# Zeroing the gate map from the mixing stage's DMA queue instead of the routing stage's

## The chip, the cores and the metric

The kernel runs on one core of a Trainium2 chip. The metric is the time of one execution on the device, in microseconds; lower is better. Before the change it is 1831.16 us, the median of three runs (1828.79 to 1844.94).

## What is computed

One layer of a streaming encoder over 512 frames and 16 meta tokens, width 1024: a token mixer (four heads of retention beside eight heads of indexer-selected attention, then one output projection), and PEER, a product-key mixture over 128 x 128 single-neuron experts. Cut to what the change touches:

```python
h += token_mixer(rmsnorm(h, norm_mix), w_in, w_uv, w_out)      # retention | attention, then @ w_out
hn = rmsnorm(h, norm_ffn)
# PEER: each token picks 16 experts in each of 8 heads
q1, q2 = split(einsum('nd,dhk->nhk', hn, w_q), 2)
s1, s2 = q1 @ sub_keys[:, 0], q2 @ sub_keys[:, 1]              # 128 scores each
eidx, gate = top16 of the sums of top16(s1), top16(s2); gate = softmax
a = einsum('nd,ned->ne', hn, u_emb[eidx])
h += einsum('ne,ned->nd', gelu(a) * gate, v_emb[eidx])
out = rmsnorm(h, norm_final)
```

## The kernel before

Matrices of f32 are multiplied in three passes: each operand is split into a high part (ScalarE copies it to a rounded type) and a low part (VectorE or GpSimd subtracts), and TensorE does high times high, high times low and low times high (lines 403 to 405, helper `three_pass`).

The program has five blocks with a barrier between them: `normed_inputs`, `project` (the input projection), `mix_rows` (retention, attention, output projection, second norm; from 244 us to 409 us of the profile), `route` (queries, top 16, gates, the first 24 of 128 tiles of expert products) and `experts` (the other tiles and the sum over them). For three of the four blocks of 128 frames the expert layer is dense: the activations of every expert are kept in DRAM (`up_acts`), and so is a dense map of gates, `gate_map`, of 128 x 128 x 384 numbers or 25 MB. It has to be zero before 384 indirect stores scatter the gates into it. POOL issues those in `experts`, after a wait for the semaphore `zeroed`. The zeros come from one tile of 128 x 384, `zeros`, which `store_zeros` writes out in 32 DMAs (`ZERO_STORES`), each of 128 x 4 x 384 numbers, 786 KB; in one of them each partition writes a piece of 6 KB, and the pieces lie 196,608 bytes apart.

All direct loads and stores are issued by SyncE (SP) into one hardware queue, in the order of the program. Where SP waits for a semaphore, all that it issues later waits too. What sets the order around the change:

- In `mix_rows` SP loads, after the tables, the 16 units of `w_out` (512 columns of 128 rows, 262 KB each) through a ring of four raw tiles, `raw_out`; unit u waits until the low part of unit u - 4 is made (`load_unit`, line 429). Then it loads the residual rows x of a block of frames (`load_rows`, line 953, 524 KB) each time the block's mixed rows have been transposed, waits until the last meta term is added (`meta_added`), and loads query tiles of `peer_wq` (524 KB each, `ts_raw_wq`, line 1518) with the last rows of x between them.
- TensorE works through 36 steps of attention, the blocks of frames in the order 3, 2, 1, 0. From step 11 on, `filler` puts pieces of the output projection between them. `project_half` needs the high and the low part of the mixed rows (`m_lo_done`) and the units of `w_out` (`lo_done`).
- ScalarE (ACT) works strictly in the order of its program. In step 11 that is: exponentials, copy of a result, the high parts of units 11 and 12 of `w_out` (line 437), the high part of the mixed rows (`high_mixed`, line 1401, `x_hi`). In step 12: exponentials, copy, units 13 and 14. After the last step: `high_mixed` of the last block, the high parts of query tiles 0 and 1 (`wq.split_hi`, line 1524), the squares of the last block's first half (`square`, line 1406), which needs x of that block, and then the high parts of the normed rows of the first three blocks (`high_normed`, line 1416). TensorE transposes normed rows (`turn_normed`, line 1114) into five PSUM banks; the sixth transpose of four waits for the first `low_normed` of VectorE (line 1323), which waits for the first `high_normed`.
- In `route` SP alternates loads of query tiles and expert tiles with stores of activations. Before the change the 32 zero fills are there, two behind each of its 16 steps.

The tile `zeros` is filled by one memset of POOL.

## Time and profile before

| | before |
|---|---|
| median of 3 runs | 1831.16 us |
| runs | 1828.79, 1831.16, 1844.94 us |
| the profiled execution, first to last instruction | 1734.2 us |
| mean granted clock of TensorE | 0.998 |
| TensorE busy | 1694.7 us, 98% |
| VectorE, ScalarE, GpSimd busy | 1105.1, 577.1, 927.0 us |
| bytes moved by DMA | 351 MB, 202 GB/s over the span |

The span is that of one profiled execution. The timed runs are about 97 us longer, because they take in what lies around the first and the last instruction. A change inside the span is added to both alike. Idle time of an engine is given in the profile with what ended it; a wait of TensorE is time of the kernel where TensorE is busy nearly all the rest of the time, a wait of another engine is only that if TensorE waits for it in turn.

### The profile page before, as it was taken

Reading aid. Unit: us, or ns where it says so; the run is one execution under the profiler, and the core shown is the slowest. Engines: PE = TensorE matmul, PEld = TensorE weight load, DVE = VectorE, ACT = ScalarE, POOL = GpSimd, SP = SyncE. Lnnn points to the kernel's source line nnn. Section 1 sums busy time; section 2 is a strip of 40 time slices with the busy share of each in tenths; the row PEclk is TensorE's granted clock in tenths of the full one; section 3 lists DMA queues with packets and bytes.
Section 4 is the critical chain, followed back from the end, with each engine's and each line's share of the span. In section 5 each row is a group of like instructions: output and inputs, shape, how many; then the busy total and the mean of one; then the engine's idle time right before and its main releaser. Section 6 shows DMA issues by size and latency. Waiting matters only on the chain.

```text
span 1734.2 us, 23540 instructions
## 1 busy us (share of the span) xinstructions
PE 1694.7 (98%) x7845; PEld 1396.2 (81%) x7845; DVE 1105.1 (64%) x2968; ACT 577.1 (33%) x929; POOL 927.0 (53%) x859
## 2 busy tenths in 40 slices
PE   7999999989999999999999999999999999999997
PEld 6877877778888878888888888888888888888886
DVE  4249968445788864444444444444688888888886
ACT  4333225343322322222222222223333333333333
POOL 3644400003354007777777777771777777777710
PEclk9999999999999999999999999999999999999999
DMA  5322231126667645444447544555999999999991
GB/s 162 105 61 58 65 65 55 42 73 219 214 236 255 218 134 145 146 145 145 145 144 244 146 146 146 146 146 165 385 390 376 370 375 361 373 375 362 378 331 49
DMA packets 182674, 351.04 MB, mean 202 GB/s; under 512 B 35600, under 2 KB 118928, under 8 KB 182448
## 3 DMA queue, kind: packets, MB, share of 16 engines
q1 hardware_dynamic: 147776, 282.74, 49.2%
q0 software_dynamic: 34816, 67.41, 10.8%
q8 instruction: 26, 0.43, 0.1%
q14 instruction: 56, 0.46, 0.1%
HBM read 289.04 MB, written 61.02 MB: 202 GB/s over the span
## 4 chain that ended last, share of the span: by engine, by line
PE 63%; DVE 0%; issue 0%; DVEq 0%; ACT 0%
PE psum L404 21%; PE psum L403 21%; PE psum L405 21%; DVE mixed L2095 0%; DVE mixed L2072 0%; DVEq L2019 0%; DVE rstd_final L815 0%; DVE rstd_final L821 0%; DVE rstd_final L817 0%; DVE rstd_final L819 0%; DVE rstd_final L813 0%; ACT rstd_final L2206 0%; DVE rstd_final L2081 0%; DVE rstd_final L2079 0%
## 5 line engine op out<-in xcount | busy, mean ns | idle before, releaser
L2281 POOL DMA_INDIRECT gate_map<-gate_total,gate_at x384 | 403.5, 1051 | 203.8 <-DVE same_expert L2026 113.2
L403 PE MATMUL psum<-x_hi,ts_hi_u 128*128 128x512 f32 x1024 | 399.1, 390 | 4.0 <-PEq L1641 2.3
L404 PE MATMUL psum<-x_lo,ts_hi_u 128*128 128x512 f32 x1024 | 398.4, 389 | 0.0
L405 PE MATMUL psum<-x_hi,ts_lo_u 128*128 128x512 f32 x1024 | 398.4, 389 | 0.0
L1529 DVE TENSOR_TENSOR ts_lo_u<-ts_raw_u,ts_hi_u 128x1024 fp32r<-128x1024 f32 x116 | 142.3, 1226 | 339.5 <-ACT ts_hi_u L1524 336.8
L403 PE MATMUL psum<-v_hi,c_hi 128*128 128x512 f32 x768 | 298.8, 389 | 0.0
L404 PE MATMUL psum<-v_lo,c_hi 128*128 128x512 f32 x768 | 298.8, 389 | 0.0
L405 PE MATMUL psum<-v_hi,c_lo 128*128 128x512 f32 x768 | 298.8, 389 | 0.0
L1560 ACT ACTIVATE ut_out_u<-psum 128x512 f32<-128x512 f32 x128 | 76.5, 598 | 494.1 <-PE psum L405 494.1
L2186 ACT ACTIVATE v_hi<-v_raw 128x1024 fp32r<-128x1024 f32 x128 | 135.8, 1061 | 312.4 <-PE psum L405 312.4
L2269 POOL DMA_INDIRECT sparse_rows<-in_peer_v,v_row x128 | 164.8, 1288 | 123.2 <-DVE sparse_more L2062 34.5
L403 PEld LDWEIGHTS psum<-x_hi,ts_hi_u 128*128 128x128 f32 x1024 | 192.3, 188 | 44.7 <-issue 2.7
L405 PEld LDWEIGHTS psum<-x_hi,ts_lo_u 128*128 128x128 f32 x1024 | 192.2, 188 | 39.8
L404 PEld LDWEIGHTS psum<-x_lo,ts_hi_u 128*128 128x128 f32 x1024 | 192.3, 188 | 39.6
L2043 DVE TENSOR_TENSOR v_lo<-v_raw,v_hi 128x1024 fp32r<-128x1024 f32 x128 | 157.0, 1226 | 79.2 <-ACT v_hi L2186 78.7
L2275 POOL DMA_INDIRECT sparse_act<-up_acts_sparse,act_at x128 | 171.6, 1341 | 40.3 <-issue 38.7
L403 PEld LDWEIGHTS psum<-v_hi,c_hi 128*128 128x128 f32 x768 | 144.2, 188 | 30.0
L404 PEld LDWEIGHTS psum<-v_lo,c_hi 128*128 128x128 f32 x768 | 144.2, 188 | 29.8
L405 PEld LDWEIGHTS psum<-v_hi,c_lo 128*128 128x128 f32 x768 | 144.2, 188 | 29.8
L1524 ACT ACTIVATE ts_hi_u<-ts_raw_u 128x1024 fp32r<-128x1024 f32 x128 | 134.5, 1052 | 0.0
L2026 DVE SCALAR_TENSOR_TENSOR same_expert<-expert,gates 128x128 f32<-128x128 f32 x384 | 112.0, 348 | 0.0
L403 PE MATMUL psum<-whi_in,h_hi 128*128 128x512 f32 (+1 forms) x280 | 109.5, 391 | 0.3 <-PEq L269 0.3
(251 smaller groups left out, 2307.5 us busy)
## 6 DMA issues: line engine op xcount, KB each, us to landing
ts_raw_u<-in_peer_u SPq DMA_DIRECT2D x128, 512.0 KB
v_raw<-in_peer_v SPq DMA_DIRECT2D x128, 512.0 KB, 6.1
gate_map<-zeros SPq DMA_DIRECT2D x32, 768.0 KB, 6.5
up_acts<-ut_out_u SPq DMA_DIRECT2D x128, 192.0 KB, 1.9
act_in<-up_acts SPq DMA_DIRECT2D x128, 192.0 KB, 6.3
gate_in<-gate_map SPq DMA_DIRECT2D x128, 192.0 KB, 6.8
raw_in<-in_w_in SPq DMA_DIRECT2D x56, 256.0 KB, 2.8
ts_raw_wq<-in_peer_wq SPq DMA_DIRECT2D x16, 512.0 KB, 6.6
```

The source lines that it names most:

```text
L403: nc.tensor.matmul(out, l_hi, r_hi, start=first, stop=False)
L404: nc.tensor.matmul(out, l_hi, r_lo, start=False, stop=False)
L405: return nc.tensor.matmul(out, l_lo, r_hi, start=False, stop=last)
L1524: nc.scalar.activation(self.hi[:, n % self.slots], self.raw[:, n % self.raws], ACT.Copy).then_inc(self.hi_done, 1)
L1529: eng_ops.tensor_tensor(self.lo[:, n % self.slots], self.raw[:, n % self.raws], self.hi[:, n % self.slots].bitcast(F32), ALU.subtract).the ...
L1560: nc.scalar.activation(self.out[:, i], self.bank[n % 2], ACT.Gelu).then_inc(self.bank_read, 1)
L2026: nc.vector.scalar_tensor_tensor(out=dn.same[:, j % 2], in0=expert[:, b], scalar=expert[:, b, j:j + 1], in1=gates[:, b].rearrange("p h k - ...
L2043: nc.vector.tensor_tensor(dn.v_lo[:, i], dn.v_raw[:, e % RAW], dn.v_hi[:, i].bitcast(F32), ALU.subtract).then_inc(v_lo_done, 1)
L2186: nc.scalar.activation(dn.v_hi[:, i], dn.v_raw[:, e % RAW], ACT.Copy).then_inc(v_hi_done, 1)
L2269: nc.gpsimd.indirect_dma_start(dn.rows[:, r], None, v_rows, bass.IndirectOffsetOnAxis(places["v_row"][:, j:j + 1], 0)).then_inc(row_in[r], 16)
L2275: nc.gpsimd.indirect_dma_start(dn.picked[:, j:j + 1], None, act_cells, bass.IndirectOffsetOnAxis(places["act_at"][:, j:j + 1], 0)).then_in ...
L2281: nc.gpsimd.indirect_dma_start(gate_cells, bass.IndirectOffsetOnAxis(places["gate_at"][:, b, j:j + 1], 0), dn.total[:, b, j:j + 1], None). ...
```

## The change

The 32 zero fills leave `route` and are issued in `mix_rows`: one behind each of the units 4 to 15 of `w_out` (12), four behind each of the three first loads of x (12), and eight more at once behind the last of these four, before the wait for `meta_added`. The tile `zeros` moves to the tiles of the mixing stage, and its memset becomes the first instruction of POOL there, ahead of the memset of `ret_scores` for which VectorE waits with its first product. SP waits for the memset ahead of unit 4. Nothing else changes; the wait for `zeroed` in `experts` stays.

```diff
@@ mix_rows, SP
+            def store_zeros(x):
+                rows = slice(x * ZERO_ROWS, (x + 1) * ZERO_ROWS)
+                sp.dma_start(gates_d[:, rows], ab["zeros"][:].unsqueeze(1).broadcast_to([P, ZERO_ROWS, DENSE])).then_inc(zeroed, 16)
...
+            sp.wait_ge(zeros_done, 1)
             for u in range(RAWRING, 2 * KT):
                 load_w(u)
+                store_zeros(u - RAWRING)
             for p in range(LAST):
                 load_rows(p)
+                for x in range(4):
+                    store_zeros(12 + 4 * p + x)
+            for x in range(24, ZERO_STORES):
+                store_zeros(x)
             sp.wait_ge(meta_added, NB)
             for t in range(2):
                 wq.load(sp, io["peer_wq"], t)
@@ mix_rows, POOL
+            nc.gpsimd.memset(ab["zeros"][:], 0.0).then_inc(zeros_done, 1)
             nc.gpsimd.memset(ret_scores[:, :, 0, :], 0.0).then_inc(padded, 1)
@@ route, SP
-            sp.wait_ge(zeros_done, 1)
             for n in range(STEPS):
                 for j in queries[n]:
                     if j + WQ_RING < SETS:
                         load_q(j + WQ_RING)
                 for t in ups[n]:
                     next_up(t)
-                for x in range(n * ZERO_STORES // STEPS, (n + 1) * ZERO_STORES // STEPS):
-                    store_zeros(x)
@@ route, POOL
-            nc.gpsimd.memset(zeros[:], 0.0).then_inc(zeros_done, 1)
```

The line numbers in the rows of before are those of the kernel before; line 1518 of before is line 1531 of the changed kernel, line 953 (loads of x) is line 959, and line 953 of the changed kernel is the new `store_zeros`.

On SP, the mixing stage before the change, from the first four units of `w_out` to the first expert tiles:

```order
L429 DMA raw_out<-in_w_out 128x512 x4
L964 DMA g_ffn_row<-g_ffn_row_d 128x1024
L429 DMA raw_out<-in_w_out 128x512 x12
L953 DMA mixed<-in_x 128x1024 x3
L1518 DMA ts_raw_wq<-in_peer_wq 128x1024 x2
L953 DMA mixed<-in_x 128x1024
L1518 DMA ts_raw_wq<-in_peer_wq 128x1024 x2
L1518 DMA ts_raw_u<-in_peer_u 128x1024 x2
```

The same place in the changed kernel, from the last of the twelve pairs of a unit and a fill on:

```order
L430 DMA raw_out<-in_w_out 128x512
L953 DMA gate_map<-zeros 128x4x384
L959 DMA mixed<-in_x 128x1024
L953 DMA gate_map<-zeros 128x4x384 x4
L959 DMA mixed<-in_x 128x1024
L953 DMA gate_map<-zeros 128x4x384 x4
L959 DMA mixed<-in_x 128x1024
L953 DMA gate_map<-zeros 128x4x384 x12
L1531 DMA ts_raw_wq<-in_peer_wq 128x1024 x2
L959 DMA mixed<-in_x 128x1024
L1531 DMA ts_raw_wq<-in_peer_wq 128x1024 x2
```

A fill now stands between every two units of `w_out` from unit 4 on, and twelve fills in a row stand between the third load of x and the first two query tiles.

On POOL, the end of the mixing stage's entry before the change (`ret_scores` is the padding for which VectorE waits, the copies gather probabilities of the meta tokens) and the begin of the routing stage:

```order
L979 UNCONDITIONAL_BRANCH
L981 MEMSET ret_scores 128x2x512
L987 COPY att_meta_probs<-att_probs 128x16 x32
L942 UNCONDITIONAL_BRANCH
L1908 UNCONDITIONAL_BRANCH
L1913 MEMSET zeros 128x384
L1529 TENSOR_TENSOR ts_lo_u<-ts_raw_u,ts_hi_u 128x1024 x2
```

The same rows in the changed kernel:

```order
L991 UNCONDITIONAL_BRANCH
L993 MEMSET zeros 128x384
L994 MEMSET ret_scores 128x2x512
L1000 COPY att_meta_probs<-att_probs 128x16 x32
L944 UNCONDITIONAL_BRANCH
L1912 UNCONDITIONAL_BRANCH
L1542 TENSOR_TENSOR ts_lo_u<-ts_raw_u,ts_hi_u 128x1024 x2
```

The memset of `zeros` has moved from the head of the routing stage to the head of the mixing stage. PE, DVE and ACT keep their order.

## Rows read from the trace of the kernel before

**Rows 1.** The page, part 1: busy time, share of the span, instructions of each engine.

```profile
PE 1694.7 (98%) x7845; PEld 1396.2 (81%) x7845; DVE 1105.1 (64%) x2968; ACT 577.1 (33%) x929; POOL 927.0 (53%) x859
```

**Rows 2.** Waits of PE, 405 to 600 us: in total, times, longest us.

```profile
PE psum L403 <- POOL ts_lo_u L1529: 1.0, 1, 1.0
PE psum L1689 <- ACT q_t L1724: 0.8, 1, 0.8
PE psum L403 <- DVE ts_lo_u L1529: 0.7, 1, 0.7
```

**Rows 3.** Timeline of POOL and DVE: start us, us, instruction, [idle before <-releaser].

```profile
244.05 0.95 POOL L981 MEMSET ret_scores<- 128x1024 f32 x1 [22.36 <-POOLq L129]
...
245.22 0.68 DVE L1205 TENSOR_TENSOR ret_scores<-psum,mixed 16x512 f32<-16x512 f32 x1 [4.73 <-PE psum L998]
...
409.28 0.42 POOL L1913 MEMSET zeros<- 128x384 f32 x1 [38.41 <-POOLq L942]
```

**Rows 4.** Timeline of SP, ACT and PE around the units of w_out.

```profile
258.53 13.33 SPq L429 DMA_DIRECT2D raw_out<-in_w_out  x7
...
299.06 6.97 SPq L429 DMA_DIRECT2D raw_out<-in_w_out  x5
...
301.66 0.63 ACT L437 ACTIVATE whi_out<-raw_out 128x512 fp32r<-128x512 f32 x1 [0.43 <-DMA raw_out<-in_w_out]
302.77 0.63 ACT L437 ACTIVATE whi_out<-raw_out 128x512 fp32r<-128x512 f32 x1 [0.48 <-DMA raw_out<-in_w_out]
303.30 0.58 ACT L1401 ACTIVATE x_hi<-psum 128x512 fp32r<-128x512 f32 x1
...
304.66 0.50 PE L403 MATMUL psum<-whi_out,x_hi 128*128 128x512 f32 x1 [1.67 <-DVE x_lo L1290]
...
309.20 0.63 ACT L1436 ACTIVATE att_probs<-att_masked,att_shift 128x400 f32<-128x400 f32 x1 [2.70 <-DVE att_shift L1250]
```

**Rows 5.** DMA view of 299 to 311 us, tile raw_out: time to landing.

```profile
DMA to landing us min/median/max: 2.5/2.7/3.1
```

**Rows 6.** Stretches with zero fills: engines' busy us, PEclk, DMA share, GB/s.

```profile
506.00:513.00 7.00, 7.00 (x37) 5.94 (x36) 2.32 (x16) 2.74 (x4) 5.78 (x10) 1.00 1.06 398
460.00:474.00 14.00, 14.00 (x72) 11.86 (x71) 7.24 (x48) 3.52 (x6) 3.33 (x5) 1.00 1.03 367
```

**Rows 7.** DMA view of 499 to 507 us: GB/s in 40 slices; time to landing.

```profile
GB/s 384 384 353 323 338 392 376 376 369 361 384 369 369 369 369 323 300 200 215 200 200 200 233 241 179 215 225 348 389 430 343 407 453 361 376 353 392 399 384 376
...
gate_map<-zeros SPq DMA_DIRECT2D x4, 768.0 KB, 10.0
```

**Rows 8.** Timeline of SP, ACT, DVE and PE at the end of the mixing stage.

```profile
362.09 0.33 SPq L953 DMA_DIRECT2D mixed<-in_x  x1
...
379.21 0.80 SPq L1518 DMA_DIRECT2D ts_raw_wq<-in_peer_wq  x2
...
382.90 2.02 ACT L1524 ACTIVATE ts_hi_wq<-ts_raw_wq 128x1024 fp32r<-128x1024 f32 x2
...
388.00 0.69 DVE L1298 TENSOR_TENSOR mixed<-psum,mixed 128x512 f32<-128x512 f32 x1 [0.74 <-PE psum L405]
388.72 0.63 ACT L1406 ACTIVATE att_probs<-mixed 128x512 f32<-128x512 f32 x1 [3.80 <-DVE mixed L1298]
...
390.71 0.66 PE L1114 MATMUL psum<-ident,att_masked 128*128 128x128 f32 x4 [0.64 <-DVE x_lo L1323]
```

**Rows 9.** DMA view of 361 to 363 us: the third load of x, to landing.

```profile
mixed<-in_x SPq DMA_DIRECT2D x1, 512.0 KB, 3.2
```

**Rows 10.** Stretches at the end of the kernel, columns as in rows 6.

```profile
1724.00:1725.00 1.00, 0.75 (x4) 0.29 (x2) 0.86 (x3) 0.17 (x1) 0.00 (x0) 1.00 0.00 0
...
1728.00:1729.00 1.00, 0.00 (x0) 0.00 (x0) 0.65 (x5) 0.18 (x1) 0.00 (x0) 0.68 1.00 373
```

**Rows 11.** Timeline of PE at the start of the kernel.

```profile
6.50 4.50 PE L367 MATMUL psum<-ident 128*128 128x128 f32 x20 [6.50 <-ACT xn_mix L333]
...
11.74 1.97 PE L362 MATMUL psum<-ident,xn_mix 128*128 128x128 f32 x16
```

More of the change, by code:

```diff
@@ L201, in program @@
                 g_row=sb("g_ffn_row", [P, D], c=stream),
+                zeros=sb("zeros", [P, DENSE], c=stream),
                 mean=sb("ffn_mean", [P, NB], c=stream),
@@ L222, in program @@
                     wq = TileStream(c3, "wq", lasting_sem, sb, psum, (0, 1), WQ_RING, WQ_RING)
-                    mix_rows(ab, st, ret, mixed, x_hi, x_lo, ws_out, ss, wq, ut, g_row_d=g_row_d, **base)
+                    mix_rows(ab, st, ret, mixed, x_hi, x_lo, ws_out, ss, wq, ut, zeroed, g_row_d=g_row_d, **base)
                     with ExitStack() as c4:
@@ L822, in refine_rstd, with mix_rows @@
     dve.wait_ge(refined, at + 5)
-def mix_rows(ab, st, ret, mixed, x_hi, x_lo, ws, ss, wq, ut, nc, io, sem, sb, psum, ident, g_row_d, **_):
+def mix_rows(ab, st, ret, mixed, x_hi, x_lo, ws, ss, wq, ut, zeroed, nc, io, sem, sb, psum, ident, gates_d, g_row_d, **_):
     decay, decay_m, ret_scores = ret["decay"], ret["decay_m"], ret["ret_scores"]
@@ L848, in mix_rows @@
     padded = sem("meta_padded")
+    zeros_done = sem("zeros_done")
     scored = sem("ret_scored")
@@ L1607, in route @@
     picked = sb("picked", [P, 2, 2, PEER_HEADS, K], c=c)
-    zeros = sb("zeros", [P, DENSE], c=c)
     gsum = sb("gate_sum", [P, NB, PEER_HEADS], c=c)
@@ L1612, in route @@
     frame = sb("frame", [P, NB], c=c)
-    zeros_done = sem("zeros_done")
     keys_in = sem("keys_in")
@@ L1649, in next_up @@
                 ut.store(sp, acts_d, acts_s, t)
-            def store_zeros(x):
-                rows = slice(x * ZERO_ROWS, (x + 1) * ZERO_ROWS)
-                sp.dma_start(gates_d[:, rows], zeros[:].unsqueeze(1).broadcast_to([P, ZERO_ROWS, DENSE])).then_inc(zeroed, 16)
             load_q(G)
```

## The prediction

> **What bounds the kernel now.** I read the page's busy times first. TensorE is busy for 1694.7 of 1734.2 us [rows 1], so the kernel is the length of TensorE's list plus its waits, and anything that a change gives or takes has to show as a wait of TensorE. Next I read the waits of TensorE in the two stages that the change touches. In the routing stage, where the fills are now, it waits for other engines three times, 1.0 + 0.8 + 0.7 = 2.5 us in all [rows 2]. So that stage already hides the fills: even if every one of these waits came from a fill, taking them all away would give 2.5 us. In the mixing stage the reader is to see a wait of TensorE for low parts, 1.67 us, that stands right behind two loads for which ScalarE waits [rows 4]. That stage has less cover. So the question is not what the fills cost where they are, but which loads they stand ahead of where they go. One queue takes SP's DMAs in order: a fill issued in a row of them lands 10.0 us after its issue [rows 7], a unit of w_out on an empty queue after 2.7 us [rows 5].
>
> **The price of a fill.** Four fills in a row are issued between 499 and 507 us [rows 7]. While they drain, from 506 to 513 us, the DMA engines are full and move 398 GB/s; over 14 us in which fills and loads alternate, 367 GB/s [rows 6]. A fill of 786 KB is 1.98 us of the queue by the first and 2.14 us by the second. I take 1.98 us, because the long train in the new place is fills alone. The fastest slice of the DMA view shows 453 GB/s, 1.74 us, and the slow stretch in it about 200 GB/s, 3.9 us [rows 7]. A query tile or a load of x (524 KB) is 1.4 us, a unit of w_out (262 KB) 0.7 us.
>
> A page of the Trainium skill gives another rate: "DMA: Bandwidth & Descriptors", section "Where 436 GB/s comes from", puts the ceiling of the ports at about 435 GB/s, but says that HBM binds at about 358 GB/s for one core. By 358 GB/s a fill would be 2.2 us, and the sum below 13 x 0.22 = 2.9 us larger. The 398 GB/s of rows 6 is above that limit, so I stay with the row.
>
> **The change part by part.**
>
> *The memset ahead of the padding.* It is 0.42 us [rows 3] and now stands before the memset of ret_scores, which starts at 244.05 us and takes 0.95 us, to 245.00. VectorE starts its first product at 245.22 us, so there are 0.22 us at most between them. VectorE starts about 0.4 us later, and TensorE, which needs its products to free banks, follows. Bounds 0 and 0.4; I take **+0.4 us**.
>
> *Units 4 to 10 with fills behind them.* SP issues these seven from 258.53 us on, within 13.33 us, each when a raw tile is free, and the next one only at 299.06 us [rows 4], when the copy of unit 7 is done. Seven units and seven fills are 7 x (0.7 + 1.98) = 19 us of the queue, over by about 285 us, some 10 us before units 7 to 10 are copied. Units 5 and 6, copied earlier, have one fill ahead of them each, 2 us, and before them stand other copies and sums of ScalarE. Nothing.
>
> *Units 11 to 15.* Here SP issues five loads from 299.06 us, each the moment that its raw tile is free, and ScalarE waits for them as they land, at 301.66 and 302.77 us [rows 4]. With a fill between units 11 and 12, unit 12 lands at 301.66 + 1.98 + 0.7 = 304.3 instead of 302.8, or 1.6 to 1.7 us late with the other rate. ScalarE works in order: behind unit 12 stands x_hi (303.30 us), behind that VectorE's x_lo, and TensorE already stands idle for it until 304.66 us [rows 4]. So the whole delay passes to TensorE: **+1.7 us**. Units 13 and 14 gather 2 and 3 fills. Unit 14 lands at 301.66 + 3 x (1.98 + 0.7) = 309.7 us and its copy ends at 310.3, while the next exponential, at 309.20 us before [rows 4], is due at 310.9 by then. So they only just hide. If fills also slow at the change from write to read, as in the dip of rows 7, this term is 2.6 us; by the fastest slice it is 1.3 us.
>
> *The first two loads of x.* They queue behind one or two fills, are wanted 10 us later, and the four fills behind each (8 us) drain before the next at 362.09 us. Nothing.
>
> *Twelve fills ahead of the query tiles.* The third load of x is issued at 362.09 us [rows 8] and lands 3.2 us later, at 365.3 [rows 9]. Behind it come 12 x 1.98 = 23.8 us of fills, to 389.1 us. Query tiles 0 and 1 are wanted at 382.90 us, x of the last block at 388.00 us [rows 8]. In the queue behind the fills they land at 390.5, 391.9 and 393.3 us. ScalarE is held at the copies of the two tiles, and VectorE at the sum with x. What is queued there: VectorE's add at 393.3, ScalarE's square 0.72 us later, and 0.63 us later the first high part of normed rows, at 394.7 instead of 389.35 us (388.72 + 0.63 [rows 8]). TensorE's sixth transpose, at 390.71 us, waits for exactly that through x_lo [rows 8]. So TensorE moves by **+5.4 us**. Both sides of this difference move by the terms above alike, so they add. With 2.14 us a fill it is 7.3 us, with 1.74 us it is 2.5. It is nothing only below 1.53 us a fill, faster than any slice.
>
> *The clock.* That wait makes TensorE idle for 0.64 + 5.4 = 6.0 us. At the end of the kernel its last matmul runs until 1724.75 us, and the granted clock falls from 1.00 in the slice from 1728 us (0.68 means that it fell at about 1728.4) [rows 10]: 3.6 us without work, and it went from 2.4 to 1.2 GHz. So I expect it to fall here. At the start of the kernel, after 6.5 us of nothing, 20 transposes take 4.50 us, 0.225 each, where 16 later ones take 1.97 us, 0.123 each [rows 11]. The difference, 20 x 0.102 = **+2.0 us**, is my price. Bounds: 0 if it doesn't fall; 3.2 us if all 12 matmuls behind the transposes run at half speed (12 x 0.23 + 4 x 0.1).
>
> *What the routing stage gets back.* 32 x 1.98 = 63 us of queue time leave it, but it is covered. The wait for GpSimd's ts_lo_u, 1.0 us [rows 2], stands behind loads that queue behind fills; the other two stand elsewhere (the copies of the first queries, and the crowded VectorE at the end). I take **-1.0 us**; bounds 0 and -2.5. The memset that leaves there was not waited for.
>
> *The sum.* 0.4 + 1.7 + 5.4 + 2.0 - 1.0 = 8.5 us. The span goes from 1734.2 to 1742.7 us. The profiled span lies 97 us under the median of the runs; I add the difference to that: **1839.7 us**. The lowest of all bounds, 0 + 1.3 + 2.5 + 0 - 2.5, is +1.3 us (1832.5 us), the highest, 0.4 + 2.6 + 7.3 + 3.2, +13.5 us (1844.7 us).
>
> **The rivals.**
>
> *The loads pass the fills.* If loads don't wait behind fills in the queue, the two large terms and the clock vanish: 0.4 - 1.0 = -0.6 us, 1830.6 us. Against it speaks the 10 us to landing of a fill in a row [rows 7] against 2.7 us of a lone load [rows 5]. For it: data of later transfers may overlap the tail of earlier ones. The Trainium skill, "DMA: Bandwidth & Descriptors", section "Queues, rings and completion order", says that descriptors are consumed in ring order but that a later one may finish its write first; by it only the tail of a transfer is passed, and this rival would be as unlikely as I have it.
>
> *The routing stage was held up more than its waits show.* All 2.5 us of rows 2 go, and the mixing stage hides the fills: -2.5 us or, with the memset, -2.1 us, 1829.1 us. This needs the first rival as well.
>
> *The fills are slow in their new place.* In the dip of rows 7, 2 us long, the engines are full and move 200 GB/s. If a train of twelve fills runs at that rate, a fill is 3.9 us: the train costs 12 x 1.95 = 23.4 us more, unit 12 comes 2 us later, and the sum is 8.5 + 25.4 = +34 us, 1865 us. It decides from 2.73 us a fill (288 GB/s) on: 13 x 0.75 = 9.8 us more make 18.3 us, 1% of the time. For it: the pieces of the fill lie 196,608 bytes apart, and nothing in the trace has more than four fills in a row. Against it: those four ran at 398 GB/s for 7 us [rows 6]. The Trainium skill has a rule that speaks for it, in "DMA: Bandwidth & Descriptors", section "Latency and other measured facts": copies with a row pitch of a large power of two fell to 207 GB/s at 512 KiB. The pitch here is 192 KiB; by that rate a fill is 3.8 us and the kernel would take about 1863 us.
>
> **How the numbers follow.** The forecast has 0.70. It rests on one queue in order, which the landing times show, and on a rate that was read over 7 us. That the loads pass the fills has 0.12, the relief of the routing stage 0.05, slow fills 0.11, and 0.02 is for the rest. The range from 1830 to 1849 us takes in the forecast's own range, the first rival and the milder part of the third, and what runs of one kernel differ by. A measurement of this kernel can tell about 1% from no change, 18 us. Slower by over 1% is the slow fill: 0.11. Faster by over 1% no case reaches: 0.02. Within 1%: 0.87.
>
> **What would show it.** In the changed profile: ScalarE's wait for the unit of w_out behind the first fill near 302 us, 1.5 to 2 us longer, and TensorE's wait for x_lo behind it, near 3.3 us instead of 1.67. At the end of the stage a wait of ScalarE of over 7 us for ts_raw_wq, a wait of VectorE for x, and TensorE idle for about 6 us before a transpose of normed rows, with a granted clock under 1 behind it. In the routing stage the 25 MB are gone from the queue, and TensorE's waits fall from 2.5 to 1.5 us. The prediction is wrong if the query tiles land before 385 us with the fills ahead of them (queue order), if the twelve fills take more than 33 us (rate), or if TensorE finds another wait that is longer than these.

## The result and the profile after

| | before | changed |
|---|---|---|
| median of 20 runs | 1831.38 us | 1844.62 us |
| lowest and highest run | 1820.23, 1846.26 us | 1827.70, 1856.32 us |
| ratio to before, with its 95% interval | | 1.0054 (1.0030 to 1.0078) |
| profiled execution | 1734.2 us | 1843.5 us |
| TensorE busy, mean granted clock | 1694.7 us, 0.998 | 1733.0 us, 0.978 |
| first load of the mixing stage, keys' load of the routing stage | 244.04, 409.66 us | 244.22, 424.68 us |

By the ratio the changed kernel is slower by 0.54%, 9.9 us (5.5 to 14.3); the two medians alone lie 13.2 us apart, inside the same interval. That is within 1%, inside the range from 1830 to 1849 us, and 1.4 us (by the medians 4.7 us) from the forecast of +8.5. But the two profiled spans are 109 us apart. So either the medians or the spans must not be set against each other, and that had to be cleared up first.

The page of the changed kernel, part 1, and its waits of TensorE over the whole span, longest first:

```profile
PE 1733.0 (94%) x7845; PEld 1415.1 (77%) x7845; DVE 1106.2 (60%) x2968; ACT 576.0 (31%) x929; POOL 926.1 (50%) x859
```

```profile
PE psum L404 <- DVE ts_lo_u L1542: 50.2, 22, 5.2
PE psum L404 <- ACT ut_out_u L1573: 9.1, 3, 3.1
PE psum L1127 <- DVE x_lo L1336: 7.4, 1, 7.4
PE psum L368 <- ACT xn_mix L334: 6.9, 1, 6.9
PE psum L404 <- DVE x_lo L1303: 6.5, 6, 4.1
```

Two groups belong to the change: the single wait of 7.4 us for the normed rows (x_lo, line 1336) and the 4.1 us for x_lo of line 1303. Of the 50.2 us 49.5, and all of the 9.1 us, stand behind 600 us among the expert tiles (ts_lo_u, ut_out_u), 175 us and more behind the keys' load of the routing stage.

The mixing stage, around the units of w_out: timeline of SP, ScalarE and TensorE.

```profile
300.63 0.33 SPq L430 DMA_DIRECT2D raw_out<-in_w_out  x1
...
303.38 0.63 ACT L438 ACTIVATE whi_out<-raw_out 128x512 fp32r<-128x512 f32 x1 [0.57 <-DMA raw_out<-in_w_out]
306.69 0.63 ACT L438 ACTIVATE whi_out<-raw_out 128x512 fp32r<-128x512 f32 x1 [2.69 <-DMA raw_out<-in_w_out]
307.23 0.58 ACT L1414 ACTIVATE x_hi<-psum 128x512 fp32r<-128x512 f32 x1
...
308.59 0.79 PE L404 MATMUL psum<-whi_out,x_hi 128*128 128x512 f32 x1 [4.09 <-DVE x_lo L1303]
309.18 0.63 PE L405 MATMUL psum<-wlo_out,x_hi 128*128 128x512 f32 x1
```

Against [rows 4], ScalarE waits 2.69 us instead of 0.48 us for unit 12, which has the first fill ahead of it, and TensorE 4.09 us instead of 1.67 us. The second matmul behind the wait takes 0.63 us where the same one takes 0.39 us from 311.7 us on: the granted clock is 0.55 from 308 to 310 us, and 1.00 from 312 us on.

The end of the stage, timeline of SP, ScalarE, VectorE and TensorE, then the stretches behind the wait (columns as in [rows 6]):

```profile
367.79 18.48 SPq L953 DMA_DIRECT2D gate_map<-zeros  x12
386.31 5.16 SPq L1531 DMA_DIRECT2D ts_raw_wq<-in_peer_wq  x2
...
399.16 1.06 ACT L1537 ACTIVATE ts_hi_wq<-ts_raw_wq 128x1024 fp32r<-128x1024 f32 x1 [9.18 <-DMA ts_raw_wq<-in_peer_wq]
401.73 0.69 DVE L1311 TENSOR_TENSOR mixed<-psum,mixed 128x512 f32<-128x512 f32 x1 [0.25 <-DMA mixed<-in_x]
404.44 1.11 PE L1127 MATMUL psum<-ident,att_masked 128*128 128x128 f32 x4 [7.39 <-DVE x_lo L1336]
```

```profile
400.00:402.00 2.00, 0.00 (x0) 0.00 (x0) 1.50 (x2) 1.28 (x2) 0.00 (x0) 0.59 0.65 262
402.00:406.00 4.00, 1.56 (x6) 1.47 (x7) 2.73 (x5) 3.54 (x8) 0.00 (x0) 0.50 0.51 135
```

ScalarE stands 9.18 us at the copy of query tile 0, which it began at 382.90 us before [rows 8]. VectorE's last add waits for x, TensorE for what comes of both, and the granted clock is 0.50, the lower of its two levels, 1.2 GHz. The keys' load of the routing stage goes out 15.0 us later than before.

The routing stage, 176 us from its begin in the changed kernel:

```profile
424.00:600.00 176.00, 173.14 (x824) 144.93 (x825) 139.33 (x805) 55.27 (x80) 72.56 (x88) 1.00 0.35 114
```

The same 176 us before, 409 to 585:

```profile
409.00:585.00 176.00, 173.17 (x824) 144.92 (x825) 136.98 (x805) 55.74 (x80) 72.78 (x89) 1.00 0.74 257
```

The queue moves 114 instead of 257 GB/s, and TensorE has done the same work in the same time.

### The profile page after: what moved, and what is told of

Its sections match the earlier page's. It is cut to its first block, busy times and chain, and to the rows that moved or that the text cites. A ratio compares the mean times of both kernels' runs of the same rounds, so it can differ in the third digit from the quotient of the medians.

```text
span 1843.5 us, 23540 instructions
## 1 busy us (share of the span) xinstructions
PE 1733.0 (94%) x7845; PEld 1415.1 (77%) x7845; DVE 1106.2 (60%) x2968; ACT 576.0 (31%) x929; POOL 926.1 (50%) x859
## 4 chain that ended last, share of the span: by engine, by line
PE 51%; another core or an unknown queue 6%; issue 3%; ACT 3%; DVE 2%; ACTq 0%; DVEq 0%
PE psum L406 17%; PE psum L404 17%; PE psum L405 17%; ACT ts_hi_u L1537 2%; DVE ts_lo_u L1542 1%; ACT ut_out_u L1573 0%; DVE mixed L2098 0%; ACTq L1572 0%; DVE mixed L2075 0%; DVE same_expert L2029 0%; DVEq L2022 0%; DVE rstd_final L816 0%; DVE rstd_final L822 0%; DVE rstd_final L818 0%
## 5 line engine op out<-in xcount | busy, mean ns | idle before, releaser
L404 PE MATMUL psum<-x_hi,ts_hi_u 128*128 128x512 f32 x1024 | 411.8, 402 | 62.6 <-DVE ts_lo_u L1542 50.2
L405 PE MATMUL psum<-x_lo,ts_hi_u 128*128 128x512 f32 x1024 | 408.3, 399 | 1.5 <-issue 1.4
L406 PE MATMUL psum<-x_hi,ts_lo_u 128*128 128x512 f32 x1024 | 407.6, 398 | 1.6 <-issue 1.6
L404 PEld LDWEIGHTS psum<-x_hi,ts_hi_u 128*128 128x128 f32 x1024 | 197.6, 193 | 116.0 <-ACT ut_out_u L1573 53.0
L406 PEld LDWEIGHTS psum<-x_hi,ts_lo_u 128*128 128x128 f32 x1024 | 198.0, 193 | 45.9 <-issue 3.4
L405 PEld LDWEIGHTS psum<-x_lo,ts_hi_u 128*128 128x128 f32 x1024 | 198.1, 193 | 41.7 <-issue 0.9
L2272 POOL DMA_INDIRECT sparse_rows<-in_peer_v,v_row x128 | 158.5, 1238 | 126.0 <-DVE sparse_more L2065 38.6
```

What stands on the lines that cost most here:

```text
L404: nc.tensor.matmul(out, l_hi, r_hi, start=first, stop=False)
L405: nc.tensor.matmul(out, l_hi, r_lo, start=False, stop=False)
L406: return nc.tensor.matmul(out, l_lo, r_hi, start=False, stop=last)
L2272: nc.gpsimd.indirect_dma_start(dn.rows[:, r], None, v_rows, bass.IndirectOffsetOnAxis(places["v_row"][:, j:j + 1], 0)).then_inc(row_in[r], 16)
```

## A measure that the runs gave

Every profile shows three instants on SP: the first load of the mixing stage (decay_m, about 244 us), the third load of x (about 362) and the keys' load (sub_keys) at the head of the routing stage. They cut the execution into A (first load to third x), B (third x to keys) and the rest. All profiles can be read in them, in us:

| run | A | B | A + B | rest | time, median | ratio to before |
|---|---|---|---|---|---|---|
| before, first profile | 118.05 | 47.57 | 165.62 | 1324.54 | | |
| e1_before | 119.35 | 49.14 | 168.49 | 1324.53 | 1739.4 | 0.9998 (0.9989 to 1.0007) |
| e3_units_early | 117.92 | 58.05 | 175.97 | 1324.50 | 1747.4 | 1.0044 (1.0030 to 1.0057) |
| e2_tail_back | 122.56 | 47.56 | 170.12 | 1324.58 | 1741.8 | 1.0013 (1.0004 to 1.0022) |
| e5_after | 122.55 | 58.02 | 180.57 | 1324.54 | 1751.7 | 1.0070 (1.0056 to 1.0083) |
| changed, first profile | 123.18 | 57.28 | 180.46 | 1418.82 | | |
| e4_hidden | 119.96 | 49.20 | 169.16 | 1326.10 | 1741.7 | 1.0010 (1.0001 to 1.0019) |
| e6_hidden_one_each | 119.40 | 49.18 | 168.58 | 1324.54 | 1738.9 | 1.0000 (0.9991 to 1.0009) |
| e9_tail_8 | 119.36 | 49.21 | 168.57 | 1324.57 | 1740.3 | 0.9999 (0.9990 to 1.0008) |
| e8_gap_busy | 122.61 | 55.99 | 178.60 | 1324.57 | 1750.0 | 1.0062 (1.0048 to 1.0075) |
| e7_tail_20 | 117.68 | 75.85 | 193.53 | 1407.27 | 1862.6 | 1.0145 (1.0074 to 1.0215) |
| e11_unit_gap_busy | 121.33 | 47.54 | 168.87 | 1409.68 | 1832.5 | 1.0006 (0.9975 to 1.0036) |
| e12_idle_filled | 117.72 | 47.54 | 165.26 | 1423.25 | 1833.9 | 0.9994 (0.9957 to 1.0030) |
| e13_before_idle_filled | 117.97 | 47.55 | 165.52 | 1439.60 | 1851.6 | 0.9962 (0.9932 to 0.9993) |

The first four experiments ran on one chip, e5, e6, e8 and e9 on a second, e7, e11 and e12 on a third, e13 on a fourth. Before itself had a median of 1740.0, 1740.4, 1833.4 and 1858.4 us on them. What lies ahead of A, from the first instruction on, is 243.3 to 244.8 us long in all of them, a scatter of 1.5 us that is in the times and not in A + B.

## Experiments

### The kernel before again

No edit.

> The kernel before, profiled a second time and timed against itself. The ratio should be 1.000 within about 0.003: this is the size of a difference that means nothing. Theory: the 97 us between the profiled execution of before (1734.2 us) and its runs (median 1831) are stalls of the experts' stage that this one execution escaped, since each run of the changed kernel lasts only 1.8 us more than its span. Then this profile shows a span near 1829, TensorE waiting for the gelu and the low parts of the expert tiles between 600 and 1400 us as in the changed kernel, and the mixing stage as before: first load 244.1, third load of x 362, first load of the routing stage 409.3. Rival: the stalls come with the fills in the mixing stage. Then TensorE waits about 2 us in all in 600 to 1400 here and the span is near 1734.

The guess was wrong and the answer better. Before takes 1739.4 us here, and its profile has a span of 1736.3 us beside a time of 1738.1 us: what lies around the span is 1.8 us. The rest of the execution is 1324.53 us, the 1324.54 of the first profile. Between 600 and 1400 us TensorE waits once:

```profile
PE psum L403 <- PEq L1641: 2.2, 1, 2.2
```

So the 97 us between the profiled execution of before and its runs are not around the span. That profile was taken where the experts' stage doesn't stall, and the runs, to judge by their times, where it does. The profile of the changed kernel has a rest of 1418.82 us, which holds the stalls. Its 109 us over before's span are 94.3 us of this and 14.8 us of A + B.

A + B is 2.9 us longer here than in the first profile. Two falls of the clock make it, behind waits of 1.7 us that both executions have. Stretches of e1_before:

```profile
292.00:294.00 2.00, 1.73 (x11) 1.73 (x12) 0.83 (x5) 1.97 (x4) 0.00 (x0) 0.74 0.00 0
294.00:296.00 2.00, 2.00 (x7) 1.48 (x6) 0.89 (x3) 1.62 (x6) 0.20 (x1) 0.50 0.00 0
...
378.00:380.00 2.00, 1.63 (x5) 1.11 (x5) 0.00 (x0) 1.98 (x8) 0.00 (x0) 0.58 0.00 0
380.00:382.00 2.00, 2.00 (x6) 1.25 (x5) 0.93 (x3) 0.86 (x2) 0.00 (x0) 0.57 0.17 16
```

In the first profile of before the clock is 1.00 in all four. So A has two levels without any late load, 117.7 to 118.1 without the fall near 292 and 119.4 with it, and B two, 47.6 without the fall near 380 and 49.2 with it. Every profile without a late load shows one of each, save for A of e4.

### The tail alone and the rest alone

e2_tail_back: the last twelve fills go back to the routing stage, with a zero tile of their own there.

```diff
-            for x in range(24, ZERO_STORES):
-                store_zeros(x)
...
+                for x in range(n * 12 // STEPS, (n + 1) * 12 // STEPS):
+                    store_zeros(20 + x)
```

(The four fills behind the third load of x go back too.)

> The changed kernel with its last twelve fills (behind the third load of x, ahead of the query tiles) issued in the routing stage again; the other twenty stay. Theory: the twelve hold the query tiles back, and that with the clock that falls behind it is 9.7 of the 15.0 us by which the routing stage starts late. So it starts at about 414.6 here (before 409.3, after 424.3), TensorE's 7.4 us wait for the normed rows goes back to about 1, and the time is 3 to 6 us above before (ratio 1.002 to 1.003). Rival, the time goes by the fills in the stage and not by their place: 20 of 32 give 1.0034 and a start at 418.7. Rival, the stalls of the experts' stage carry the difference: ratio 1.005 whatever the start.

The routing stage's first load goes out at 414.54 us, as expected, and TensorE's wait for the normed rows is 0.6 us. B is 47.56, A 122.56. The ratio, 1.0013 (1.0004 to 1.0022), is a little under the 1.002 to 1.003 of the expectation and excludes both rivals, 1.0034 and 1.005.

e3_units_early: the six fills of units 10 to 15 go out together behind unit 10.

```diff
-                store_zeros(u - RAWRING)
+                for x in (range(6, 12) if u == 10 else [u - RAWRING] if u < 10 else []):
+                    store_zeros(x)
```

> The changed kernel with the six fills between and behind units 10 to 15 of w_out issued together behind unit 10, 14 us before unit 11's slot comes free; the twelve ahead of the query tiles stay. Theory: the units no longer land late, TensorE's wait for x_lo falls from 4.1 to about 1.7 us, and the third load of x goes out at 362.3 to 363.5 (before 362.1, after 367.4). The tail stays whole, so the routing stage starts at about 419 to 420 and the ratio to before is about 1.005 times two thirds, 1.0035 to 1.005. Rival, the lateness of the third x load comes from the clock that fell at 290 to 300 and not from the fills behind: then x goes out at 366 or later here too.

A is 117.92, so the late third load of x in the changed kernel comes from the fills among units 11 to 15. The rival, the clock that fell at 290 to 300 us, has a small part in it: e3_units_early does not have that fall, and e1_before, which has it, is 1.3 us longer in A than the first profile of before. The changed kernel's A is 5.1 us longer. B is 58.05, as long as with all of the change. The longest waits of TensorE in the stage:

```profile
PE psum L1128 <- DVE x_lo L1337: 8.2, 1, 8.2
...
PE psum L404 <- DVE x_lo L1304: 3.9, 6, 1.5
```

### The changed kernel on an undisturbed chip

> The changed kernel again, on the chip of the runs beside it. Theory, the parts add: the twelve fills alone (e3_units_early) cost 7.5 us, the other part (e2_tail_back) 2 to 2.4 us, so the time is 9 to 10 us over before, ratio 1.0052 to 1.0057 where before lasts about 1740. Rival: the 15.0 us by which the routing stage began late in the first profile are the cost, ratio 1.0086. Where before lasts about 1831 the same 9 to 10 us make 1.005 to 1.0055.

It is 1751.7 us, by the ratio 12.2 us over before (9.7 to 14.4), by the medians 11.3: between the two expectations. The ratios of the parts don't add to it (2.3 + 7.7 us), but the stages do once the falls of the clock are counted. From e1_before to e5_after A grows by 3.20 and B by 8.88, 12.1 in all. Against the first profile of before, which has neither fall, it is 14.9. What the change costs depends on the falls that before would have had.

e8_gap_busy (below) has the late units as well and the same A, 122.61 us, though it has the fall near 292 and e5_after has not. The two executions get there by different ways. The stretches from 292 to 298 and from 306 to 314 us, first of e5_after, then of e8_gap_busy:

```profile
292.00:298.00 6.00, 4.24 (x31) 3.66 (x31) 4.32 (x18) 5.06 (x11) 0.72 (x2) 1.00 0.00 0
306.00:314.00 8.00, 6.74 (x20) 5.21 (x21) 2.72 (x5) 2.52 (x6) 0.20 (x1) 0.57 1.06 397
```

```profile
292.00:298.00 6.00, 5.39 (x29) 4.73 (x30) 3.27 (x14) 4.12 (x11) 0.20 (x1) 0.72 0.00 0
306.00:314.00 8.00, 6.63 (x30) 5.46 (x31) 3.34 (x8) 3.30 (x10) 0.20 (x1) 0.79 1.06 398
```

With the fall near 292 the wait for x_lo ends 1.3 us later (63.7 instead of 62.5 us from the first load), and the clock behind the wait is low for a shorter time. So the late units cost 4.5 us where nothing else fell (118.05 to 122.55) and 3.3 us where the fall near 292 is there anyhow (119.35 to 122.61), or 3.8 us in the first profile of the changed kernel, whose wait is 0.6 us longer. B with the tail is much the same in this: 58.05 with the fall near 380 (e3_units_early), 58.02 without it (e5_after). The fall shortens the wait behind the fills, 8.2 instead of 9.2 us, because the queue sets its end, and from the end of the wait to the keys' load it is 20.3 instead of 20.8 us. Why the clock stays low longer in one execution than in the other wasn't asked.

### What the clock costs behind the two waits

e8_gap_busy: the changed kernel with 26 matmuls for nothing ahead of the wait of the sixth transpose.

```diff
+                    if n == 5:
+                        for _ in range(26):
+                            nc.tensor.matmul(psum[:, 0, :], x_hi[:, 0, 0:P], ws.hi[:, 0], start=True, stop=True)
                     if n >= 5:
                         pe.wait_ge(n_lo_done, n - 4)
```

> The changed kernel with 26 extra matmuls of 128x512 (6 us of work, results unused) in TensorE's queue ahead of the transposes for which it waits 7.4 us. Theory: the clock that fell to 0.5 behind the wait costs 2 us and is kept; the time is 1.5 to 2.5 us under e5_after, ratio to before about 1.004. The granted clock is 1.00 in the 10 us behind the wait, and the wait itself shrinks to about 1.4 us. Rival, the clock does not fall for want of work: it falls again and the time is that of e5_after.

B falls from 58.02 to 55.99 us and TensorE's wait to 1.4 us, as expected, and the median falls by 1.7 us. The intervals of the two ratios overlap, so it is the stage that shows it. The stretches behind the wait, first of e5_after, then of e8_gap_busy:

```profile
404.00:410.00 6.00, 5.43 (x18) 4.53 (x19) 4.69 (x8) 2.32 (x5) 0.00 (x0) 0.62 0.10 40
```

```profile
404.00:410.00 6.00, 6.00 (x32) 5.52 (x31) 4.80 (x12) 2.55 (x6) 0.00 (x0) 1.00 0.36 118
```

From the end of the wait to the keys' load it is 18.94 us in e8_gap_busy and 18.9 to 19.0 us in both profiles of before, against 20.79 us in e5_after, 20.2 to 20.3 in the first profile of the changed kernel and in e3_units_early, and 21.35 in e7_tail_20. So the clock behind the tail's wait costs 1.3 to 2.4 us, 1.9 in e5_after; the rest of the 2.03 us is that the data came 0.2 us earlier. The ratio is 1.0062 and not 1.004, because e5_after was over my expectation too; the difference of the two is what was asked for.

e11_unit_gap_busy: e2_tail_back with 13 such matmuls ahead of the first projection.

```diff
+                if p == 0 and half == 0 and r == 0:
+                    pe.wait_ge(ws.lo_done, 1)
+                    for _ in range(13):
+                        nc.tensor.matmul(psum[:, 1, :], ws.hi[:, 0, 0:P], ws.hi[:, 0], start=True, stop=True)
                 pe.wait_ge(m_lo_done, 2 * p + r + 1)
```

> The kernel of e2_tail_back (twenty fills in the mixing stage, twelve in the routing stage) with 13 extra matmuls of 128x512 (3 us of work, results unused) ahead of the first projection, where TensorE waited 3.6 us for x_lo. Theory: 1.3 of the 3.2 us that the late units cost are the clock that falls to 0.5 behind this wait; the extra work keeps it, so that the third load of x goes out 121.2 us after the stage's first load (e2: 122.6) and the clock from 306 to 314 is 1.00. Rival: the third load goes out at 122.5 again, since the wait alone is the cost.

A is 121.33 us instead of 122.56, and the clock from 306 to 314 us is 1.00, where e5_after has 0.57. But this execution has the fall near 292 (0.72 from 292 to 298 us), and e2_tail_back has not. Against e8_gap_busy, which has it too, the work in the gap saves 1.3 us; this is the price of the clock behind the wait there. What stays, 121.33 - 119.4, is 1.9 us, the growth of the wait from 1.6 to 3.5 us. Without the fall near 292 the same 1.9 us leave 4.5 - 1.9 = 2.6 us for the clock. The time can't show any of it: the ratio is 1.0006 (0.9975 to 1.0036), on a chip where runs scatter by 36 us.

### Where the tail begins to cost, and its slope

Both keep twelve fills behind units 4 to 10 as e3_units_early, and vary how many stand between the third load of x and the query tiles: 8 in e9_tail_8, 20 in e7_tail_20 (the remaining twelve, or none, behind the first two loads of x).

```diff
+            load_rows(2)
+            for x in range(32 - n, ZERO_STORES):
+                store_zeros(x)
```

> Only eight fills between the third load of x and the query tiles; the other 24 where nothing waits for them (one behind each of units 4 to 9, six behind unit 10, six behind each of the first two loads of x). Theory, the tail costs by how far its fills outlast the 18.3 us that were free: 8 fills by 2.1 us are 17.1 us, so the query tiles land no later than before and the ratio is 1.000 to 1.001. Rival, each fill ahead of the query tiles costs its own 0.6 us (7.5 over 12): plus 5 us, ratio 1.003.

> Twenty fills between the third load of x and the query tiles, the other twelve behind units 4 to 10 where nothing waits. Theory, one queue drains the fills ahead of the query tiles at a steady rate and whatever outlasts the free 18.3 us is paid in full: eight fills more than in e3_units_early are 8 x 2.1 = 17 us more, so 7.5 + 17 = 24.5 us over before, ratio 1.014, and TensorE's wait for the normed rows is about 25 us. Rival, the fills overlap with the tiles behind them once the queue is deep: less than 12 us more, ratio under 1.011.

ScalarE at query tile 0, e9_tail_8, then e7_tail_20:

```profile
385.79 2.05 ACT L1541 ACTIVATE ts_hi_wq<-ts_raw_wq 128x1024 fp32r<-128x1024 f32 x2
```

```profile
411.62 1.06 ACT L1541 ACTIVATE ts_hi_wq<-ts_raw_wq 128x1024 fp32r<-128x1024 f32 x1 [25.32 <-DMA ts_raw_wq<-in_peer_wq]
```

Eight fills cost nothing (B 49.21, the 49.14 of e1_before). Twelve cost 8.9 us, twenty 26.7 us: 17.8 us for eight fills, 16.7 of them that the tiles land later and 1.1 that the clock is low for longer behind the wait. TensorE's wait for the normed rows is 23.5 us, where I expected about 25. The time of e7_tail_20 has four runs, and its ratio, 1.0145 (1.0074 to 1.0215), takes in the 1.014 of the theory and the rival's 1.011; the stage excludes the rival. From the third load of x to the copy of tile 0 it is 32.5 us with twelve (361.45 to 393.98 in e3_units_early) and 49.2 us with twenty (362.38 to 411.62): 16.7 / 8 = 2.09 us a fill, 376 GB/s. The other three profiles with twelve fills have 31.8 to 32.0 us there, and by them a fill is 2.2 us. e7_tail_20's train in two stretches:

```profile
364.00:378.00 14.00, 11.05 (x62) 8.97 (x60) 4.60 (x15) 5.09 (x20) 0.40 (x2) 0.99 1.03 380
378.00:398.00 20.00, 15.25 (x64) 11.88 (x64) 6.12 (x12) 3.37 (x8) 0.00 (x0) 0.84 1.04 366
```

### All fills in the mixing stage, none ahead of a load that is wanted

e4_hidden has two fills behind each of units 4 to 9, e6_hidden_one_each one each and six behind unit 10; both have ten behind each of the first two loads of x.

```diff
-                for x in range(4):
-                    store_zeros(12 + 4 * p + x)
-            for x in range(24, ZERO_STORES):
-                store_zeros(x)
+                if p < 2:
+                    for x in range(10):
+                        store_zeros(12 + 10 * p + x)
```

> All 32 fills in the mixing stage, but none ahead of a load that is waited for: two behind each of units 4 to 9, ten behind the first and ten behind the second load of x. Theory: only the memset's 0.2 us is left; the routing stage starts at 409.5 to 410.5, and the ratio is 1.000 within the noise (0.998 to 1.002). Rival, filling 8 MB in this stage costs by its bandwidth wherever it stands: the start is near 424 and the ratio 1.005. Rival, the routing stage gives something back when no fill runs in it: TensorE's span from the first routing load to 176 us later holds more than the 173.2 us of work of before, and the ratio is below 0.999.

> All 32 fills in the mixing stage, at most one behind each of units 4 to 9, six behind unit 10, ten behind each of the first two loads of x. Theory: the 1.0 to 1.8 us of e4_hidden came from two fills ahead of units 5 to 10 (TensorE waited 1.8 us at 270 to 290 there that it doesn't wait in before); with one each nothing is late, and only the memset's 0.2 us is left: ratio 1.0001, within 0.9995 to 1.0008. Rival: filling in this stage costs 1.8 us anyhow, ratio 1.001 again.

e6 is at 1.0000. A and B are those of e1_before to 0.05 us. So in these places neither the fills nor the memset cost anything. Two fills ahead of each unit do cost something: e4's A is 119.96 us with a clock of 1.00 from 290 to 300 us, 1.9 us over the level of 118.05 that goes with it. TensorE has waits in e4 that e1 and e6 don't have, 1.5 us of the 1.9:

```profile
PE psum L1033 <- DVE att_peak L1259: 0.9, 1, 0.9
...
PE psum L1062 <- DVE att_dv_meta_t L1277: 0.6, 1, 0.6
```

Its rest is 1.6 us longer than all others on these two chips, and this is the clock again. Near 640 us TensorE waits 2.2 us for its own sequencer. Behind this wait e4's clock falls, where the other eight profiles with an unstalled experts' stage, which all have the wait, have 1.00:

```profile
640.00:644.00 4.00, 3.44 (x8) 2.73 (x9) 1.22 (x1) 0.00 (x0) 0.00 (x0) 0.57 0.60 181
```

### Keeping the clock up

e12_idle_filled is e6_hidden_one_each with six matmuls for nothing ahead of each of the two waits of 1.7 us for att_out_t. e13_before_idle_filled is before with the same, all fills in the routing stage.

```diff
                 p, h = divmod(i, DSA_HEADS)
+                if i in (5, UNITS - 1):
+                    pe.wait_ge(ws.lo_done, 1)
+                    for _ in range(6):
+                        nc.tensor.matmul(psum[:, 3 if i == 5 else 4, :], ws.hi[:, 0, 0:P], ws.hi[:, 0], start=True, stop=True)
                 pe.wait_ge(out_copied, i + 1)
```

> The kernel of e6_hidden_one_each (all 32 fills in the mixing stage, nothing late) with six extra matmuls of 128x512 (1.4 us of work, results unused) ahead of each of the two waits of 1.7 us for att_out_t, near 292 and 378 us. Theory: behind each of these waits the clock falls in some executions and not in others, at 1.4 and 1.6 us each; with the engine busy it falls in none. The stage is then 165.7 us long from its first load to the keys' load (e1_before 168.5, the first profile of before 165.6), and the time is 2 to 3 us under before, ratio 0.9983 to 0.9989. Rival: the falls come from elsewhere, the stage is 168.5 long and the ratio is 1.000.

> The kernel before, all fills in the routing stage, with the same twice six extra matmuls (results unused) ahead of the two waits of 1.7 us for att_out_t. Theory: the clock stays up behind both waits and the mixing stage lasts 165.3 to 165.7 us from its first load to the keys' load, as in e12_idle_filled and the first profile of before, against 168.5 in e1_before; the place of the fills makes no difference when nothing waits for them. Where before lasts about 1740 us the time is 2 to 3 us under it, ratio 0.9983 to 0.9989. Where before lasts about 1833 its own spread hides this, and the ratio is 0.998 with 1.000 inside its interval; then the stage's length alone can tell. Rival: with the fills in the routing stage the routing stage gives something up, and the rest of the execution behind the keys' load is longer than 1324.6 us on the faster chip.

A + B is 165.26 us in e12 and 165.52 us in e13 (244.78 to 410.30), the length that only the first profile of before had. Of the twelve profiles without this work six fell near 292 us and eight near 380 us, so that four gaps in a row without a fall would come by luck in about 3 of 100 cases. e13 in the two places:

```profile
290.00:300.00 10.00, 9.15 (x56) 6.83 (x55) 8.28 (x28) 7.62 (x17) 1.03 (x3) 1.00 0.00 0
376.00:384.00 8.00, 7.75 (x39) 5.94 (x38) 4.15 (x12) 5.63 (x14) 0.00 (x0) 1.00 0.37 126
```

The times can't say as much. e12 ran where before varies from 1819 to 1855 us: ratio 0.9994, with 0.9983 inside its interval. e13 came out at 1851.6 against 1858.4 us, ratio 0.9962 (0.9932 to 0.9993). That is faster than before by 7 us, more than the 3 us which the stage can explain, so part of it is scatter or something in the experts' stage. Neither ran on a chip where before takes 1740 us, where 3 us would stand out.

## Why the prediction came out as it did

**The chain of argument held.** One queue in order, the two places at which a load stands behind fills, and the waits named (ScalarE at unit 12 and at the query tiles, VectorE at x, TensorE at x_lo and the sixth transpose) are all in the trace. Moving the fills off those two places takes the whole cost away (e6_hidden_one_each); each place alone gives its own part (e2, e3).

**The memset, +0.4.** It cost nothing: A of e6_hidden_one_each, with the memset in front, is 119.40 against 119.35 us. I took the upper of my bounds.

**Units 4 to 10, nothing.** Right for one fill each (e6). Two each are already seen (e4).

**Units 11 to 15, +1.7.** The wait grew by 2.4 us in the first profile and by 1.9 us in e5_after, as the mechanism wanted. What the step left out is the clock behind this wait: another 1.3 us where the clock has just fallen near 292 as well (e11_unit_gap_busy against e8_gap_busy), 2.6 us where it has not. I had priced a fall only at the long wait. The term is 3.2 us against e1_before and 4.5 us against the first profile of before.

**Twelve fills, +5.4.** The wait of TensorE grew from 0.6 to 9.2 us in e5_after, 8.2 in e3_units_early and 7.4 us in the first profile, so 7 to 8.6 us. The rate was a part of it: 2.09 us a fill instead of 1.98, 12 x 0.11 = 1.3 us. By the prediction's own sum with 2.09 us, tile 0 comes 3.2 + 12 x 2.09 + 1.4 = 29.7 us behind the issue of the third load of x. e3_units_early shows 32.5 us. The other 2.8 us are no larger with twenty fills (e7_tail_20). With eight there is room for 1.2 us at most, since the copy of tile 0 begins without a wait 22.5 us after the issue (e9_tail_8). About 0.8 us of it is a dip where the fills end and the tiles begin, the dip of [rows 7] that I had counted only in the bounds of the units' term. e3_units_early:

```profile
388.00:391.00 3.00, 3.00 (x24) 2.62 (x22) 0.00 (x0) 0.00 (x0) 0.00 (x0) 1.00 1.04 268
```

The remaining 2 us aren't explained. The rate of 367 GB/s, which I had for the sum's upper bound, was the nearer one.

**The clock, +2.0.** It fell, and it cost 1.9 us in e5_after and 1.3 us in the first profile of the changed kernel. The price had a weak source. I took it from 20 slow transposes at the start of the kernel [rows 11], but in that trace the granted clock reads 1.00 from the first slice on, so nothing there shows that the clock made them slow. That it met the measured size is luck. The four transposes behind the wait show the price in its place: 1.11 us at a clock of 0.50 in e5_after, 0.66 us at 1.00 in e8_gap_busy.

**The routing stage, -1.0.** Nothing came back. The wait of 1.0 us for GpSimd's ts_lo_u [rows 2] is still there, 1.0 to 1.1 us, with no fill on the queue, and the rest of the execution is 1324.5 us with all fills in the routing stage (e1), twelve of them (e2) or none (e5, e6). The row showed a wait behind loads; that these were late on account of the fills was my guess.

**The sum.** In the stage's length it is 3.2 + 8.9 = 12.1 us against e1_before, where I had 8.5. Where before takes 1740 us the time shows 12.2 us, where it takes 1831 us 9.9 (5.5 to 14.3), which agrees with both. That the forecast met the result to 1.4 us is in part luck. The units with the clock behind them were too small by 1.5 us, the tail with its clock by 1.5 us, the relief of the routing stage was 1.0 us that did not come, and only the memset, 0.4 us too large, went the other way. Against an execution of before without falls the gap is 14.9 to 8.5. The interval of the result takes in 8.5 and 12.1 us alike.

**The 97 us.** I said that they lie around the first and last instruction. That is wrong: 1.8 us do. They are stalls in the experts' stage, which come on some chips and not on others, so the profile on which the sum was made and the runs to which it was added belong to different conditions. It did no harm, since the change lies ahead of that stage and the rest doesn't depend on it, but nothing in the argument had shown that.

**The rivals.** Loads don't pass fills: from twelve to twenty of them tile 0 lands later by 2.1 to 2.2 us with each fill. The routing stage had nothing to give. Slow fills didn't come: the train runs at 366 to 380 GB/s. Here the trace also decides between the rules of the Trainium skill, page "DMA: Bandwidth & Descriptors". The 207 GB/s that its section "Latency and other measured facts" gives for a pitch of 512 KiB were not met at the 192 KiB here. The limit of 358 GB/s in "Where 436 GB/s comes from" would make a fill 2.2 us. The long train's 366 to 380 GB/s lie above it, but nearer to it than the 398 GB/s by which I had set it aside.

## What to carry to other kernels

A bulk store costs what it delays, and that is decided by the loads behind it on its queue: 32 fills cost nothing where every wanted load was ahead of them, 8.9 us for twelve ahead of two tiles. Eight in the same place cost nothing, and from twelve to twenty each one cost 2.2 us; where between eight and twelve the cost begins wasn't measured. Before you set a profiled span against a median, look for the runs' own spans; a gap of 5% between them is another condition of the chip, not an overhead. And cut the execution at fixed instructions: the stage's length repeated to 0.1 us (168.49, 168.57, 168.58) in executions with the same falls of the clock, where times scattered by 3 to 36 us. Ask for the granted clock first, though, because one fall more or less moves the same length by 1.4 to 1.6 us.

## What the runs showed that I had not expected

A wait of only 1.6 to 1.8 us can cost as much again. Behind the two waits for att_out_t the granted clock falls to 0.50 (1.2 GHz) in some executions and stays at 1.00 in others, at 1.4 and 1.6 us each. Six matmuls for nothing in the gap kept it in both executions that had them. Together the two falls are 3.0 us, of the 5.2 us by which runs of before differ on the two chips with 1740 us (1736.4 to 1741.6). What decides it from one execution to the next wasn't found. With the longer waits, 3.5 us and more for x_lo and 7.4 us and more for the normed rows, it fell in all the executions that left the gap empty, four of each.

The same kernel takes 1740 us on two chips, 1833 and 1858 us on two others. There TensorE waits in the experts' stage for low parts of expert tiles, as the changed kernel's 50.2 us above, and its granted clock is 0.96 in the mean from 600 to 1300 us in that profile. The kernel before does the same where it takes 1858 us (e13_before_idle_filled waits 45.9 us for them), so the stalls don't come with the change. ScalarE's gelu of the first profile of the changed kernel, from 1069 us on:

```profile
1069.20 0.60 ACT L1573 ACTIVATE ut_out_u<-psum 128x512 f32<-128x512 f32 x1 [7.32 <-PE psum L406]
1075.01 0.60 ACT L1573 ACTIVATE ut_out_u<-psum 128x512 f32<-128x512 f32 x1 [4.26 <-PE psum L406]
1085.78 0.60 ACT L1573 ACTIVATE ut_out_u<-psum 128x512 f32<-128x512 f32 x1 [9.22 <-PE psum L406]
1087.22 0.59 ACT L1573 ACTIVATE ut_out_u<-psum 128x512 f32<-128x512 f32 x1
```

The same in e5_after, two in a row of a series that stays like this:

```profile
1071.34 0.60 ACT L1573 ACTIVATE ut_out_u<-psum 128x512 f32<-128x512 f32 x1 [3.89 <-PE psum L406]
1076.78 0.60 ACT L1573 ACTIVATE ut_out_u<-psum 128x512 f32<-128x512 f32 x1 [3.89 <-PE psum L406]
```

One every 5.44 us in the second; in the first, the third comes 10.8 us behind the second and the fourth right after it: a whole product late, and what follows in ScalarE's queue with it. Why it does so on some chips isn't settled; no experiment went there.
